# Two weight splits at each layer norm boundary move from GpSimd to VectorE

## The chip, the cores and the metric

One core of one Trainium2 chip runs the whole kernel. The time is the device time of one execution in microseconds, as the median of several runs; smaller is better. TensorE does the matmuls and transposes, VectorE, ScalarE and GpSimd the elementwise work, SyncE issues the transfers.

## The reference

Four layers on 256 tokens of width 1024, all in float32. Each layer is a half-step SwiGLU feed-forward (width 2816), a token mixer (stick-breaking attention, sliding window attention, dilated attention, and stick-breaking again), a second feed-forward, and a gated per-layer input embedding (PLE). The first three end with a layer norm:

```python
for i in range(DEPTH):                       # DEPTH = 4
    x = _layernorm(a * x + 0.5 * _swiglu(x, ffn1_w_in[i], ffn1_w_out[i]), ln_g[i, 0], ln_b[i, 0])
    mix = ...                                # mixer number i % 3
    x = _layernorm(a * x + mix, ln_g[i, 1], ln_b[i, 1])
    x = _layernorm(a * x + 0.5 * _swiglu(x, ffn2_w_in[i], ffn2_w_out[i]), ln_g[i, 2], ln_b[i, 2])
    x = x + jax.nn.sigmoid(x @ ple_w_gate[i]) * (p[i] @ ple_w_proj[i])
```

with `_layernorm(x) = (x - mean) * rsqrt(var + 1e-5) * g + b` over the 1024 columns.

## The kernel before

**Tiles and units.** The 256 tokens are two tiles of 128 (`t` = 0 and 1). Weights are streamed as 730 units of 128 x 1024 numbers (512 KB each) through rings of six slots. To multiply float32 precisely, each unit is split: ScalarE copies `raw` to `wh` in the shorter type fp32r (L446, counted by `hi_done`), then `wl = raw - wh` is computed (L678 on VectorE, counted by `lo_done`). The activations have the same two parts, `xh` and `xl`. TensorE then does three matmuls for each product, wh*xh, wl*xh and wh*xl (L935 to L937). A unit is six matmuls of 512 columns for each tile in most places.

**Stages.** `stages` lists 16 stages in order: ffn1, mixer, ffn2 and PLE for each layer. Each engine runs its own program over them; the order of the work on each is written out by hand, and semaphores tie them. ScalarE splits up to four units (`LEAD`) ahead of the stage that TensorE is in. SyncE loads unit u when `lo_done` says that the slot of unit u - 6 has been split; the loads of the norm's g and b (`norm_load`) stand in the same queue, and wait until the last x of the norm before has been written.

**A boundary.** Behind 12 of the 16 stages (all but PLE) stands a layer norm. On VectorE it is the function `boundary`. For each tile: `residual` (L730) adds the stage's result in two halves of 512 columns, `center` computes the mean (L736) and subtracts it (L741), and `scale` (L750) multiplies by rstd and adds b, one instruction for each half. Between them ScalarE squares and sums (L495), and GpSimd raises to the power -0.5 (L414, L416). `stream_t` makes the next stage's operand: TensorE transposes the half (L978, four transposes), ScalarE copies it to `xh` (L452) and VectorE subtracts to `xl` (L685).

**TensorE at the boundary.** A stage's last four units and the next stage's first four are run by tile. The transposes of tile 0's new x stand before the very last unit of the old stage (tile 1, unit 4 of 4). Behind it come units 0, 1 and 2 of the new stage for tile 0, then the transposes of tile 1's new x, then unit 3 for tile 0, then the four units for tile 1. VectorE's `residual` for tile 1's second half needs that very last unit.

**Who splits here.** Of the four units ahead, `split(2)` in front of `boundary` does units 0 and 1 of the next stage. Units 2 and 3 are split by GpSimd: behind tile 0's rstd its program subtracts `wh` from `raw` for both (L421), once ScalarE has copied them (`split(2)` behind the square of tile 0) and the units before are counted. VectorE skips their numbers (`st["u"] += 2`), and the first split that it does afterwards waits until GpSimd's are counted (`after_pool`). At a PLE stage VectorE does all of them.

Of the kernel before, what the change touches and what calls it, by code (L numbers as in the profile page):

```python
# [20 lines left out]
F32 = mybir.dt.float32  # L21
F32R = mybir.dt.float32r
I32 = mybir.dt.int32
ALU = mybir.AluOpType
# [15 lines left out]
RING = 6  # L40
LEAD = 4
# [34 lines left out]
def steps_of(l):  # L76

    kind = mixer_of(l)
    if kind == "swa":
        return [("q", 0, 0), ("kv", 0, 0), ("q", 1, 0), ("attn", 0, 0), ("attn", 1, 0)]  # L80
    steps = []
    for hh in range(2):
        for g in range(NG if kind == "dil" else 1):
            steps += [("q", hh, g), ("k", hh, g), ("v", hh, g)]
        steps.append(("attn", hh, 0))
    return steps
# [9 lines left out]
def units_of(step):  # L96
    return 2 if step == "kv" else 4


def build_program(nc, A, out):  # L100
    ctx = ExitStack()
    with ctx:
        def sb(name, shape, dt=F32):
            return ctx.enter_context(nc.sbuf_tensor(name, shape, dt))


        raw = sb("raw", [P, RING, UW])
        wh = sb("wh", [P, RING, UW], F32R)
        wl = sb("wl", [P, RING, UW], F32R)
# [78 lines left out]
        def semaphore(name):  # L188
            return ctx.enter_context(nc.semaphore(name))

        landed = [semaphore(f"landed{s}") for s in range(RING)]
        hi_done = semaphore("hi_done")
        lo_done = semaphore("lo_done")
# [37 lines left out]
        stages = []  # L231
        u = 0
        for l in range(DEPTH):
            for kind in ("ffn1", "mix", "ffn2", "ple"):
                n = {"ffn1": 66, "ffn2": 66, "ple": 10, "mix": 8 + sum(units_of(s[0]) for s in steps_of(l) if s[0] != "attn")}[kind]
# [12 lines left out]
        for kind, l, i, u0, n in stages:  # L248
# [49 lines left out]
            if i + 1 < NST:  # L298
                note_stream("x", i + 1)

        norm_index = {i: 3 * l + ("ffn1", "mix", "ffn2").index(kind) for kind, l, i, _, _ in stages if kind != "ple"}

        def wait(eng, sig, *key):
            eng.wait_ge(sig.sem, sig.at(*key))
# [101 lines left out]
        @block.gpsimd  # L406
        def _(pool):
            pool.memset(mhalf[:], -0.5).then_inc(mh_done, 1)
            pool.wait_ge(mh_done, 1)
            for kind, l, i, u0, n in stages:  # L410
                if kind != "ple":
                    for t in range(NT):
                        wait(pool, ssq_done, i, t)
                        pool.tensor_scalar(veps[:, t, :], ssq[:, t, :], 1.0 / D, EPS, ALU.mult, ALU.add).then_inc(mh_done, 1)  # L414
                        pool.wait_ge(mh_done, 2 + 2 * norm_index[i] + t)
                        pool.tensor_tensor(rstd[:, t, :], veps[:, t, :], mhalf[:], ALU.pow).then_inc(rstd_done.sem, 1)  # L416
                        if t == 0:
                            for u in (u0 + n + LEAD - 2, u0 + n + LEAD - 1):
                                pool.wait_ge(hi_done, u + 1)
                                pool.wait_ge(lo_done, u)  # L420
                                pool.tensor_tensor(wl[:, u % RING, :], raw[:, u % RING, :], wh[:, u % RING, :].bitcast(F32),  # L421
                                                   ALU.subtract).then_inc(lo_done, 1)


        @block.scalar
# [231 lines left out]
        def _(dve):  # L657
            st = {"u": 0, "own": 0}

            def own(ins):  # L660

                st["own"] += 1
                ins.then_inc(own_dve, 1)
                dve.wait_ge(own_dve, st["own"])

            after_pool = {u0 + n + LEAD for kind, l, i, u0, n in stages if kind != "ple"}

            def split(n=1, du=0):

                for _ in range(n):  # L670
                    u = st["u"]
                    if u >= UNITS:
                        return
                    st["u"] += 1
                    dve.wait_ge(hi_done, u + 1 + du)
                    if u in after_pool:
                        dve.wait_ge(lo_done, u)
                    dve.tensor_tensor(wl[:, u % RING, :], raw[:, u % RING, :], wh[:, u % RING, :].bitcast(F32),  # L678
                                      ALU.subtract).then_inc(lo_done, 1)

            def stream_t(key, i, t):

                for c in range(2):
                    wait(dve, th_done, key, i, t, c)
                    dve.tensor_tensor(xl[:, 4 * c:4 * c + 4, t, :], ps[:, 2 * t + c, :].rearrange("p (k m) -> p k m", m=P),  # L685
                                      xh[:, 4 * c:4 * c + 4, t, :].bitcast(F32), ALU.subtract).then_inc(tl_done.sem, 1)
# [16 lines left out]
            def ffn(i):  # L703
                split(8)
                hidden(i, 0, BLK)
                with dve.Fori(0, NJ - 1) as r:
                    split(3, r * 12)
                    hidden_t(i, 0, 4, 0, r)
                    split(9, r * 12)
                    hidden(i, 1, BLK, r)  # L710
                st["u"] += 12 * (NJ - 2)
                split(2)
                hidden_t(i, NJ - 1, 4, 0)
                split(2)
                hidden(i, NJ, 256)
                split(2)
                hidden_t(i, NJ, 2, 4)

            def y_wait(kind, i, t, c):

                if t == 0:
                    wait(dve, acc_ready, "y", i, c)
                else:
                    dve.wait_ge(w_used, ends["y", i] - (0 if c else 1 if kind == "ple" else 2))

            def residual(kind, i, t, c):

                y_wait(kind, i, t, c)
                h = slice(c * BLK, (c + 1) * BLK)
                return dve.scalar_tensor_tensor(x[:, t, h], x[:, t, h], ALPHA, ps[:, 4 + 2 * t + c, :], ALU.mult, ALU.add,  # L730
                                                accum_out=rsum[:, t, c:c + 1])

            def center(i, t, ins):

                own(ins)
                dve.tensor_scalar(nmean[:, t, :], rsum[:, t, 0:1], rsum[:, t, 1:2], -1.0 / D, ALU.add, ALU.mult).then_inc(mean_done.sem, 1)  # L736
                wait(dve, mean_done, i, t)
                if t == 0:
                    dve.wait_ge(g_landed, 16 * (norm_index[i] + 1))
                    dve.wait_ge(b_landed, 16 * (norm_index[i] + 1))  # L740
                dve.scalar_tensor_tensor(xn[:, t, :], x[:, t, :], nmean[:, t, :], gb[:, 0, :], ALU.add,  # L741
                                         ALU.mult).then_inc(xn_done.sem, 1)

            def scale(i, t):

                wait(dve, xn_done, i, t)
                wait(dve, rstd_done, i, t)
                for c in range(2):
                    h = slice(c * BLK, (c + 1) * BLK)
                    dve.scalar_tensor_tensor(x[:, t, h], xn[:, t, h], rstd[:, t, :], gb[:, 1, h], ALU.mult,  # L750
                                             ALU.add).then_inc(x_new.sem, 1)

            def embed(i, t):
                for c in range(2):
                    if c == 0:
                        wait(dve, sig_done, i, t)
                    y_wait("ple", i, t, c)
                    h = slice(c * BLK, (c + 1) * BLK)
                    own(dve.tensor_tensor(eg[:, t, h], eg[:, t, h], ps[:, 2 * t + c, :], ALU.mult))
                    dve.tensor_tensor(x[:, t, h], x[:, t, h], eg[:, t, h], ALU.add).then_inc(x_new.sem, 1)  # L760

            def boundary(kind, i):
                more = i + 1 < NST
                if kind == "ple":
                    for t in range(NT):
                        embed(i, t)
                        if t == 0:
                            split(2)
                        if more:
                            stream_t("x", i + 1, t)  # L770
                    return
                residual(kind, i, 0, 0)
                center(i, 0, residual(kind, i, 0, 1))
                scale(i, 0)
                residual(kind, i, 1, 0)
                stream_t("x", i + 1, 0)
                center(i, 1, residual(kind, i, 1, 1))
                st["u"] += 2
                scale(i, 1)
                stream_t("x", i + 1, 1)  # L780

# [577 lines left out]
```

## Time and profile before

| what | value |
|---|---|
| median of 3 runs | 2451.0 us (2448.92 to 2451.81) |
| the profiled execution, first to last instruction | 2447.3 us |
| what lies around that span, against the median | 3.7 us |
| TensorE busy in the span | 2363.5 us, 97% |
| VectorE, ScalarE, GpSimd busy | 1344.2, 1104.6 and 77.8 us |
| mean granted clock of TensorE | 0.967 of full speed |

The profile gives times in us from the start of the span. For the profiled execution only its span is recorded; the three runs are timed as a whole. Busy time of TensorE counts matmuls in flight, also at a lower clock.

### The profile page before, as it was taken

What the parts mean: (1) busy time and instruction counts of PE and PEld (TensorE: products, weight loads), DVE (VectorE), ACT (ScalarE), POOL (GpSimd) and SP (SyncE); (2) the same over time, 40 slices, a digit from 0 to 9 for tenths busy, and PEclk for the clock granted to TensorE, in tenths of its full rate; (3) what the DMA queues carried; (4) which work ended last, traced back from release to release, by engine and by line L of the source; (5) the groups of instructions that cost most, each with busy time, mean ns of one, the idle gap of its engine ahead of it and who ended that gap; (6) DMA issues with size and microseconds to landing.
All of it is one profiled execution on the core that took longest, in us unless ns stands there. A gap on an engine that the chain in (4) does not pass through costs nothing.

```text
span 2447.3 us, 29751 instructions
## 1 busy us (share of the span) xinstructions
PE 2363.5 (97%) x11220; PEld 1943.7 (79%) x11220; DVE 1344.2 (55%) x1634; ACT 1104.6 (45%) x1411; POOL 77.8 (3%) x77
## 2 busy tenths in 40 slices
PE   8999999999999899999999999999999999999998
PEld 7887778878888578878887888787887887777887
DVE  5556355556456465556456655645556546446545
ACT  5444554435344544445344344444444444554443
POOL 0001010010001010010001000000001000001001
PEclk9999999999999589999999999999999999999999
DMA  8555336546654136546655515415554654435562
GB/s 288 187 182 171 97 129 204 179 153 203 201 180 155 35 130 197 180 150 208 196 181 171 180 62 162 148 52 197 186 187 147 207 188 146 164 112 181 174 200 86
DMA packets 212917, 401.21 MB, mean 164 GB/s; under 512 B 12369, under 2 KB 30929, under 8 KB 212689
## 3 DMA queue, kind: packets, MB, share of 16 engines
q1 hardware_dynamic: 212816, 399.83, 50.5%
q8 instruction: 69, 1.13, 0.2%
q14 instruction: 32, 0.25, 0.0%
HBM read 398.73 MB, written 1.05 MB: 163 GB/s over the span
## 4 chain that ended last, share of the span: by engine, by line
PE 92%; DVE 5%; ACT 1%; issue 1%; POOL 0%; DMA 0%; SPq 0%; DVEq 0%; POOLq 0%; ACTq 0%
PE ps L935 27%; PE ps L936 26%; PE ps L937 26%; PE ps L978 5%; DVE x L750 3%; PE ps L1071 2%; PE ps L1101 2%; PE ps L1125 1%; PE ps L1136 1%; DVE wl L678 1%; PE ps L1128 0%; DVE x L730 0%; PE ps L1147 0%; PE ps L1126 0%; ACT arena L495 0%
## 5 line engine op out<-in xcount | busy, mean ns | idle before, releaser
L678 DVE TENSOR_TENSOR wl<-raw,wh 128x1024 fp32r<-128x1024 f32 x706 | 845.3, 1222 | 482.0 <-ACT wh L446 477.4
L446 ACT ACTIVATE wh<-raw 128x1024 fp32r<-128x1024 f32 x730 | 758.0, 1060 | 613.1 <-PE ps L937 595.9
L935 PE MATMUL ps<-wh,xh 128*128 128x512 f32 (+1 forms) x2320 | 890.5, 384 | 5.2 <-DVE xl L685 5.0
L936 PE MATMUL ps<-wl,xh 128*128 128x512 f32 (+1 forms) x2320 | 880.1, 379 | 0.0
L937 PE MATMUL ps<-wh,xl 128*128 128x512 f32 (+1 forms) x2320 | 879.6, 379 | 0.0
L935 PEld LDWEIGHTS ps<-wh,xh 128*128 128x128 f32 x2320 | 441.6, 190 | 87.2 <-DVE xl L685 6.7
L937 PEld LDWEIGHTS ps<-wh,xl 128*128 128x128 f32 x2320 | 440.2, 190 | 82.5
L936 PEld LDWEIGHTS ps<-wl,xh 128*128 128x128 f32 x2320 | 441.2, 190 | 78.8
L935 PE MATMUL ps<-wh,hth 128*128 128x512 f32 x704 | 282.2, 401 | 0.0
L937 PE MATMUL ps<-wh,htl 128*128 128x512 f32 x704 | 278.0, 395 | 0.0
L936 PE MATMUL ps<-wl,hth 128*128 128x512 f32 x704 | 277.9, 395 | 0.0
L935 PEld LDWEIGHTS ps<-wh,hth 128*128 128x128 f32 x704 | 134.4, 191 | 33.2 <-issue 5.8
L937 PEld LDWEIGHTS ps<-wh,htl 128*128 128x128 f32 x704 | 134.4, 191 | 28.7
L691 DVE TENSOR_TENSOR htl<-ps,hth 128x512 fp32r<-128x512 f32 (+1 forms) x96 | 57.6, 642 | 179.6 <-ACT hth L459 179.6
L936 PEld LDWEIGHTS ps<-wl,hth 128*128 128x128 f32 x704 | 134.6, 191 | 25.9
L459 ACT ACTIVATE hth<-ps 128x512 fp32r<-128x512 f32 (+1 forms) x96 | 48.7, 561 | 205.5 <-PE ps L978 205.5
L700 DVE SCALAR_TENSOR_TENSOR arena<-arena,ps 128x512 f32<-128x512 f32 (+1 forms) x96 | 57.5, 640 | 141.0 <-PE ps L937 141.0
L978 PE MATMUL ps<-consts,arena 128*128 128x128 f32 x724 | 105.6, 289 | 5.9 <-DVE arena L849 5.9
L978 PEld LDWEIGHTS ps<-consts,arena 128*128 128x128 f32 x724 | 87.9, 149 | 23.6 <-issue 11.9
L750 DVE SCALAR_TENSOR_TENSOR x<-arena,rstd,gb 128x512 f32<-128x512 f32 x48 | 84.9, 1808 | 23.7 <-POOL rstd L416 23.7
L978 PE MATMUL ps<-consts,x 128*128 128x128 f32 x256 | 43.9, 311 | 55.4 <-DVE x L750 50.6
L452 ACT ACTIVATE xh<-ps 128x512 fp32r<-128x512 f32 x64 | 36.5, 596 | 120.1 <-PE ps L978 119.9
(85 smaller groups left out, 1179.2 us busy)
## 6 DMA issues: line engine op xcount, KB each, us to landing
raw<-in_ffn_w_in SPq DMA_DIRECT2D x352, 512.0 KB, 4.6
raw<-in_ffn_w_out SPq DMA_DIRECT2D x176, 512.0 KB, 4.6
raw<-in_dil_w_in SPq DMA_DIRECT2D x72, 512.0 KB, 4.6
raw<-in_sb_w_in SPq DMA_DIRECT2D x48, 512.0 KB, 4.6
raw<-in_ple_w_gate SPq DMA_DIRECT2D x32, 512.0 KB, 4.3
raw<-in_sb_w_out SPq DMA_DIRECT2D x16, 512.0 KB, 3.8
gb<-in_ln_g SPq DMA_DIRECT2D x12, 512.0 KB, 4.3
gb<-in_ln_b SPq DMA_DIRECT2D x12, 512.0 KB, 5.7
```

The source lines that it names most:

```text
L446: act.activation(wh[:, u % RING, :], raw[:, u % RING, :], ACT.Copy).then_inc(hi_done, 1)
L459: ins = act.activation(hth[:, at:at + n, t, :], ps[:, 2 + t, 0:n * P].rearrange("p (c m) -> p c m", m=P), ACT.Copy)
L678: dve.tensor_tensor(wl[:, u % RING, :], raw[:, u % RING, :], wh[:, u % RING, :].bitcast(F32), ALU.subtract).then_inc(lo_done, 1)
L691: ins = dve.tensor_tensor(htl[:, at:at + n, t, :], ps[:, 2 + t, 0:n * P].rearrange("p (c m) -> p c m", m=P), hth[:, at:at + n, t, :].bitca ...
L700: ins = dve.scalar_tensor_tensor(hb[:, t, 0:n], sg[:, t, 0:n], 0.5, ps[:, 2 + t, 0:n], ALU.mult, ALU.mult)
L750: dve.scalar_tensor_tensor(x[:, t, h], xn[:, t, h], rstd[:, t, :], gb[:, 1, h], ALU.mult, ALU.add).then_inc(x_new.sem, 1)
L935: pe.matmul(out_, a_h, b_h, start=start, stop=False)
L936: pe.matmul(out_, a_h, b_l, start=False, stop=False)
L937: return pe.matmul(out_, a_l, b_h, start=False, stop=stop)
L978: ins = pe.transpose(ps[:, bank + c // 4, (c % 4) * P:(c % 4 + 1) * P], src[:, at + c * P:at + (c + 1) * P], ident)
L1071: ins = pe.matmul(ps[:, bank, at:at + (t + 1) * P], qT[pb:pb + HD, g if kc is None else hh, h // 2, t * P:(t + 1) * P], kT[pb:pb + HD, g, ...
L1101: ins = pe.matmul(opair(h)[pb:pb + HD, t * P:(t + 1) * P], v, eT[:, t * ng + m, :], start=m == 0, stop=m == n - 1)
```

## The change

GpSimd keeps its two small operations for each tile, and no longer splits. VectorE takes both splits itself with the usual `split(2)`, placed behind tile 0's `stream_t` and in front of the `residual` for tile 1's second half. The wait of VectorE for GpSimd's count and the set `after_pool` go. Rings, loads, loops and the other three engines' programs stay.

```diff
@@ gpsimd
                         pool.tensor_tensor(rstd[:, t, :], veps[:, t, :], mhalf[:], ALU.pow).then_inc(rstd_done.sem, 1)
-                        if t == 0:
-                            for u in (u0 + n + LEAD - 2, u0 + n + LEAD - 1):
-                                pool.wait_ge(hi_done, u + 1)
-                                pool.wait_ge(lo_done, u)
-                                pool.tensor_tensor(wl[:, u % RING, :], raw[:, u % RING, :], wh[:, u % RING, :].bitcast(F32),
-                                                   ALU.subtract).then_inc(lo_done, 1)
@@ vector
-            after_pool = {u0 + n + LEAD for kind, l, i, u0, n in stages if kind != "ple"}
-
             def split(n=1, du=0):
...
                     dve.wait_ge(hi_done, u + 1 + du)
-                    if u in after_pool:
-                        dve.wait_ge(lo_done, u)
                     dve.tensor_tensor(wl[:, u % RING, :], raw[:, u % RING, :], wh[:, u % RING, :].bitcast(F32),
                                       ALU.subtract).then_inc(lo_done, 1)
@@ vector, boundary
                 scale(i, 0)
                 residual(kind, i, 1, 0)
                 stream_t("x", i + 1, 0)
+                split(2)
                 center(i, 1, residual(kind, i, 1, 1))
-                st["u"] += 2
                 scale(i, 1)
                 stream_t("x", i + 1, 1)
```

## Rows read from the trace of the kernel before

**Rows 1.** Page, chain that ended last, share of the span by line.
```profile
PE ps L935 27%; PE ps L936 26%; PE ps L937 26%; PE ps L978 5%; DVE x L750 3%; PE ps L1071 2%; PE ps L1101 2%; PE ps L1125 1%; PE ps L1136 1%; DVE wl L678 1%; PE ps L1128 0%; DVE x L730 0%; PE ps L1147 0%; PE ps L1126 0%; ACT arena L495 0%
```

**Rows 2.** Waits: who waited for whom, us in total, times, longest.
```profile
PE ps L978 <- DVE x L750: 50.6, 24, 2.2
```

**Rows 3.** Groups by line, GpSimd: busy us, mean ns.
```profile
L421 POOL TENSOR_TENSOR wl<-raw,wh 128x1024 fp32r<-128x1024 f32 x24 | 59.7, 2486 | 3.0
```

**Rows 4.** Timeline of VectorE, boundary at 758: start us, us.
```profile
758.24 5.67 DVE L750 SCALAR_TENSOR_TENSOR x<-arena,rstd,gb 128x512 f32<-128x512 f32 x2 [0.98 <-POOL rstd L416]
763.83 0.67 DVE L730 SCALAR_TENSOR_TENSOR x<-x,ps 128x512 f32<-128x512 f32 x1
...
764.43 0.68 DVE L685 TENSOR_TENSOR xl<-ps,xh 128x512 fp32r<-128x512 f32 x1
765.74 0.69 DVE L685 TENSOR_TENSOR xl<-ps,xh 128x512 fp32r<-128x512 f32 x1 [0.63 <-ACT xh L452]
767.68 0.69 DVE L730 SCALAR_TENSOR_TENSOR x<-x,ps 128x512 f32<-128x512 f32 x1 [1.24 <-PE ps L937]
...
770.93 1.41 DVE L750 SCALAR_TENSOR_TENSOR x<-arena,rstd,gb 128x512 f32<-128x512 f32 x2 [0.98 <-POOL rstd L416]
...
776.37 2.36 DVE L678 TENSOR_TENSOR wl<-raw,wh 128x1024 fp32r<-128x1024 f32 x2 [1.57 <-ACT wh L446]
```

**Rows 5.** Timeline of ScalarE, same boundary.
```profile
757.12 1.99 ACT L446 ACTIVATE wh<-raw 128x1024 fp32r<-128x1024 f32 x2
761.90 0.60 ACT L452 ACTIVATE xh<-ps 128x512 fp32r<-128x512 f32 x1 [2.79 <-PE ps L978]
```

**Rows 6.** Timeline of TensorE, same boundary.
```profile
758.41 0.39 PE L936 MATMUL ps<-wl,hth 128*128 128x512 f32 x1
758.64 0.39 PE L937 MATMUL ps<-wh,htl 128*128 128x512 f32 x1
761.21 0.66 PE L978 MATMUL ps<-consts,x 128*128 128x128 f32 x4 [2.18 <-DVE x L750]
763.96 1.12 PE L978 MATMUL ps<-consts,x 128*128 128x128 f32 x4 [2.10 <-DVE x L750]
764.73 0.78 PE L935 MATMUL ps<-wh,hth 128*128 128x512 f32 x1
...
767.01 0.63 PE L937 MATMUL ps<-wh,htl 128*128 128x512 f32 x1
767.44 0.63 PE L935 MATMUL ps<-wh,xh 128*128 128x512 f32 x1
...
772.24 1.04 PE L978 MATMUL ps<-consts,x 128*128 128x128 f32 x8
773.03 0.47 PE L935 MATMUL ps<-wh,xh 128*128 128x512 f32 x1
```

**Rows 7.** Timeline of GpSimd, same boundary.
```profile
758.24 5.11 POOL L421 TENSOR_TENSOR wl<-raw,wh 128x1024 fp32r<-128x1024 f32 x2
```

**Rows 8.** Stretches: length, busy by engine, TensorE's granted clock, DMA.
```profile
763.96:768.90 4.94, 4.94 (x14) 4.08 (x15) 3.00 (x8) 0.84 (x2) 0.00 (x0) 0.50 0.00 0
...
2410.72:2414.00 3.28, 3.28 (x11) 2.63 (x9) 1.76 (x5) 0.60 (x1) 0.00 (x0) 0.50 0.52 165
```

**Rows 9.** Timeline of VectorE, two other boundaries.
```profile
1843.24 5.67 DVE L750 SCALAR_TENSOR_TENSOR x<-arena,rstd,gb 128x512 f32<-128x512 f32 x2 [0.98 <-POOL rstd L416]
...
2404.57 5.67 DVE L750 SCALAR_TENSOR_TENSOR x<-arena,rstd,gb 128x512 f32<-128x512 f32 x2 [0.98 <-POOL rstd L416]
```

**Rows 10.** Timeline of TensorE, the same two boundaries, start of unit 3.
```profile
1858.26 0.47 PE L935 MATMUL ps<-wh,xh 128*128 128x512 f32 x1
...
2418.79 0.48 PE L935 MATMUL ps<-wh,xh 128*128 128x512 f32 x1
```

**Rows 11.** Timeline of TensorE, first transposes at two boundaries.
```profile
342.19 1.11 PE L978 MATMUL ps<-consts,x 128*128 128x128 f32 x4 [2.18 <-DVE x L750]
...
1086.01 0.84 PE L978 MATMUL ps<-consts,x 128*128 128x128 f32 x4 [2.18 <-DVE x L750]
```

## The prediction

> **What bounds the kernel now.** I read the chain that ended last first. It lies almost wholly on TensorE, but one VectorE line stands out in it: L750, the scaling that ends a layer norm, has 3% of the span, some 73 us, on the path [rows 1]. The waits say the same from TensorE's side: the longest thing it waits for is that line, 50.6 us in 24 waits of its transposes [rows 2]. The 24 are two at each of the 12 layer norm boundaries. No row of the waits has TensorE waiting for a split, on VectorE or GpSimd, so weights are in time everywhere. The kernel is thus TensorE plus 12 holes, and the change works exactly in these holes. GpSimd's two splits per boundary, 2.49 us each [rows 3], begin in the same instant as L750 does [rows 4, 7].
>
> **One boundary, clocked from L750.** I call 758.24 time 0 and take the boundary there for all, since the twelve look alike. VectorE's L750 is two instructions for tile 0 and takes 5.67 us for them; for tile 1, same shapes and same operation, it takes 1.41 [rows 4]. The only work present at the first and absent at the second is GpSimd's pair, 5.11 us from time 0 [rows 7]; ScalarE converts in the first case too, but only until 0.87 [rows 5]. So the two engines hinder each other by about 5.67 - 1.41 = 4.26 us.
> TensorE's last ordinary matmul starts at 0.40, and the pitch is 0.23 [rows 6]; from 0.63 it has nothing. It transposes x's first half at 2.97, the second at 5.72, runs the closing stage's last unit from 6.49, the next stage's unit 0 from 9.20, units 1 and 2 after it, tile 1's eight transposes at 14.00, and unit 3 from 14.79 [rows 6]. I use the start of unit 3 as the end of the boundary: behind it both traces hold the same work. The boundary where it came earliest has it at 2418.79 - 2404.57 = 14.22, the one where it came latest at 1858.26 - 1843.24 = 15.02 [rows 9, 10]; the mean of the twelve is 14.63.
>
> **The change part by part.**
> *GpSimd's splits go.* L750 for tile 0 then takes what tile 1's takes. Its first half is written at 0.74, the second at 1.41. From one half's end to the transposes TensorE needs 0.13 (the first half of the slow pair ends at 5.67 / 2 = 2.84; transposes at 2.97). So transposes start at 0.87 and 1.54. Four cost 0.40, half of the 0.79 that eight took [rows 6]. The closing unit starts at 1.54 + 0.40 = 1.94 instead of 6.49 and its six matmuls end at 1.94 + 6 x 0.23 = 3.32.
> The Trainium skill, SBUF — State Buffer, section "SBUF: two separate sides", says that VectorE and GpSimd share a port pair which one instruction holds to its end, and that a VectorE operation with two SBUF inputs asks for it against a GpSimd operation that reads SBUF. L750 has two such inputs, and so have the moved splits. By that rule they too would be slow beside GpSimd; by the trace GpSimd has nothing left to do from time 0 until tile 1's rstd, so neither view charges them.
> *VectorE up to the new splits.* The residual of tile 1's first half follows at 1.33 (issue is 0.08 before the pair's end) and takes 0.60 to the next issue [rows 4]. ScalarE is free at 0.87 and copies a half in 0.60, some 0.69 after its transposes begin [rows 5, 6]: 1.56 to 2.16, and, behind the second transposes, 2.23 to 2.83. VectorE's subtractions of xl (0.68 each) run at 2.18 and 2.85, and it is free at 3.46.
> *The two moved splits.* Two splits took 2.36 [rows 4], pitch 1.18. The inputs are there (ScalarE ended them at 0.87). So they run from 3.46 to 5.82. GpSimd had them done at 2.5 and 5.1; unit 2 needs the first at 3.32 + 2 x 1.38 = 6.08, where it is now done at 4.66, and unit 3 needs the second much later. Nothing waits for them on TensorE. SyncE's loads of units 8 and 9 wait for the same count, which comes up to 2.2 us later; before the stages with a norm they stand behind norm_load, which waits for tile 1's x, later still, and a PLE stage has TensorE six units away from them.
> *What stands behind them on VectorE.* This is the price. The residual of tile 1's second half could have run at about 3.4, when the closing unit ends; it now runs at 5.80. From that residual to tile 1's scale it is 3.25 (767.68 to 770.93, with ScalarE's square and GpSimd's power inside [rows 4]), so L750 starts at 9.05 and writes at 9.79 and 10.46. TensorE transposes at 9.92 and 10.59 and starts unit 3 at 10.99. It had finished unit 2 at 3.32 + 3 x 1.38 = 7.46: a new hole of about 2.4 us, owed to the splits. Without them in the way the hole would be nearly gone.
> *Removed waits.* VectorE's and GpSimd's waits for each other's split count cost nothing that a row shows; I take 0. Their upper bound is the time to release an engine, 0.13 a boundary, 1.6 in all.
> *Sum at full clock.* 14.63 - 10.99 = 3.64 a boundary, times 12 = 43.7 us.
>
> **The clock.** The boundary of before held TensorE at half of its 2.4 GHz: granted 0.50 from 763.96 to 768.90, and matmuls at a pitch of 0.43 [rows 6, 8]. That loss is inside the 14.63. After the change the first hole is gone, but the new one of 2.4 is as wide as one of the old ones (2.18). Whether one such hole alone lets the clock fall can be read where the first transposes already ran slow: 1.11 at 342.19 and 0.84 at 1086.01, against 0.66 [rows 6, 11]; that is the case at 3 boundaries (these two are the first and the last), at 9 the clock fell after the second hole. At least a quarter, then, and with a slightly wider hole more; between 0 and 12 I take 6. The price: the shortest low stretch had 3.28 us of busy TensorE at 0.50 in the row shown [rows 8], so half of it, 1.64, rounded up to 1.7 for its edges, is lost; the long one costs 4.94 / 2 = 2.5. Six falls at 1.7 are 10.2 us.
> The Trainium skill, TensorE: Matmul & The Clock Gate, Part 1, says that the gate's schedule runs free of the kernel, so that the same hole may or may not let the clock fall. The trace agrees with its 3 and 9 of 12; it is why I spread over all counts.
>
> **Result.** 43.7 - 10.2 = 33.5 us. The profiled execution spans 2447.3 us; the median of the runs is 2451.0, the 3.7 between is what lies around the span, and I leave it. 2447.3 - 33.5 = 2413.8 of span, 2417.5 us of time.
>
> **The rivals.**
> *No hole lets the clock fall.* The new hole stands alone, where the old ones came in pairs, and 9 of 12 boundaries stood the first. Then 2451.0 - 43.7 = 2407.3.
> *Every hole does.* 12 x 1.7 = 20.4 come back: 2451.0 - 43.7 + 20.4 = 2427.7; with the long fall, 12 x 2.5, 2437.3. Against it: 9 of 12.
> *The weights become the wait.* All of a stage's first loads and splits must come 3.6 us earlier beside unchanged DMA. But the loads behind norm_load hang on tile 1's x and move with it, and the first split behind the boundary ends at 19.3 (776.37 + 1.18 [rows 4]) where unit 4 is wanted at 14.79 + 5 x 1.38 = 21.7. With that slack of 2.4 used up and 1 us lost at each boundary: 2417.5 + 12 = 2429.5.
> *L750 stays slow: the slower case.* If the 5.67 came from something else than GpSimd (ScalarE's work, a bank), the splits would only be a burden. VectorE would be free at 8.11, split until 10.45, run the residual there instead of at 9.44, and all behind it would be 1.01 later: 12 x 1.01 = 12.1 slower, 2463.1. It decides once L750's pair for tile 0 stays above 1.41 + 3.64 = 5.05 us. Against it: GpSimd's 5.11 and the clean 1.41, twelve times over.
> *Nothing changes.* It needs the pair near 5.05 by chance, or a gain that TensorE gives back wholly in the stages; it is busy there without holes.
>
> **How the numbers follow.** Forecast with some falls 0.64; no fall 0.12; falls everywhere 0.12; weights 0.06; slower 0.03; nothing 0.03. The bound between a change and none is 0.2% or 4.9 us, about what this kernel's runs can tell. Faster is 0.94. The range goes from just under the rival without falls, 2405, to just over the weights' rival, 2431; it leaves out the long falls, the slower case and no change.
>
> **What would show it.** L750: 48 instructions at about 0.71 instead of 1.81, and no row of L421; L678 has 24 more, at 1.22. TensorE's transposes at the first tile wait 0.2 to 0.3 instead of 2.18 and 2.10, and at tile 1 for about 2.3, from L750. Unit 3 starts 11.0 after L750's first start. Low clock appears behind tile 1's transposes, at some boundaries. I am wrong if L750's pair for tile 0 is longer than 2, if VectorE's splits are slower than 1.2, if unit 2 waits for L678, or if holes open later in the stages.

## The result, and the profile after

| | before | changed |
|---|---|---|
| median of 4 runs, us | 2449.96 | 2412.03 |
| span of the profiled execution, us | 2447.3 | 2409.6 |
| mean granted clock of TensorE | 0.967 | 0.978 |
| mean of the 12 boundaries, L750's (now L740's) first start to unit 3, us | 14.63 | 11.01 |

The ratio is 0.9846, 95% interval 0.9832 to 0.9860: 37.9 us faster. The forecast was 2417.5 us, with a range of 2405 to 2431. Of the runs below, one of the four executions of "splits only counted" took 3325.0 us at a granted clock of 0.649, and its ratio is worked out without it.

Lines have moved: L740 is `scale` (L750 before), L668 the split (L678), L720 the residual, L731 the centering, L675 the subtraction to xl, L968 the transposes, L925 a first matmul.

The groups by line (busy us, mean ns of one; then idle before them and its releaser), the scaling before and then two lines of the changed kernel:

```profile
L750 DVE SCALAR_TENSOR_TENSOR x<-arena,rstd,gb 128x512 f32<-128x512 f32 x48 | 84.9, 1808 | 23.7 <-POOL rstd L416 23.7
```

```profile
L668 DVE TENSOR_TENSOR wl<-raw,wh 128x1024 fp32r<-128x1024 f32 x730 | 873.9, 1222 | 486.7 <-ACT wh L440 484.0 <-DVE arena L783 0.5
...
L740 DVE SCALAR_TENSOR_TENSOR x<-arena,rstd,gb 128x512 f32<-128x512 f32 x48 | 34.0, 749 | 24.0 <-POOL rstd L416 24.0
```

The mean over the 48 cases of L740 is 749 ns, where it was 1808, and the split costs the same 1222 ns with 24 more of them (706 before). No GpSimd row of the splits (L421 before) is left.

The timeline of VectorE at the same boundary as in [rows 4]; L740 now starts at 748.52:

```profile
748.52 1.42 DVE L740 SCALAR_TENSOR_TENSOR x<-arena,rstd,gb 128x512 f32<-128x512 f32 x2 [0.98 <-POOL rstd L416]
749.86 0.68 DVE L720 SCALAR_TENSOR_TENSOR x<-x,ps 128x512 f32<-128x512 f32 x1
...
750.65 1.36 DVE L675 TENSOR_TENSOR xl<-ps,xh 128x512 fp32r<-128x512 f32 x2
751.93 2.35 DVE L668 TENSOR_TENSOR wl<-raw,wh 128x1024 fp32r<-128x1024 f32 x2
754.20 0.68 DVE L720 SCALAR_TENSOR_TENSOR x<-x,ps 128x512 f32<-128x512 f32 x1
...
757.44 1.41 DVE L740 SCALAR_TENSOR_TENSOR x<-arena,rstd,gb 128x512 f32<-128x512 f32 x2 [0.98 <-POOL rstd L416]
```

Read the last three rows as one sentence: the splits run without a pause from 3.41 to 5.76 after L740's start, the residual starts at 5.68 as they end, and tile 1's L740 follows 3.24 behind the residual. Up to the residual nothing waits for anything but VectorE itself; the 3.24 hold the centering, ScalarE's square and GpSimd's power, for which VectorE waits 0.98.

TensorE at the same boundary, against [rows 6]:

```profile
749.33 1.32 PE L968 MATMUL ps<-consts,x 128*128 128x128 f32 x8
750.41 0.47 PE L925 MATMUL ps<-wh,hth 128*128 128x512 f32 x1
...
758.24 1.97 PE L968 MATMUL ps<-consts,x 128*128 128x128 f32 x8 [2.11 <-DVE x L740]
759.86 0.78 PE L925 MATMUL ps<-wh,xh 128*128 128x512 f32 x1
```

The two old holes are gone: all eight transposes of tile 0 run in one piece at 0.81, and the closing unit starts at 1.89. The new hole has 2.11 us, in front of tile 1's transposes. Here they take 1.97 us and the next matmul 0.78, as in a stretch at half clock; at another boundary, in the same view, they take 1.32 and 0.48:

```profile
2380.04 1.32 PE L968 MATMUL ps<-consts,x 128*128 128x128 f32 x8 [2.11 <-DVE x L740]
2381.12 0.48 PE L925 MATMUL ps<-wh,xh 128*128 128x512 f32 x1
```

The stretches (length, busy time by engine, granted clock, DMA) show it as a number, first behind the boundary at 1624, where the clock fell only after unit 3 had begun, then behind the one shown:

```profile
1636.00:1639.00 3.00, 3.00 (x9) 2.40 (x8) 1.32 (x2) 2.99 (x3) 0.00 (x0) 0.54 1.03 289
759.00:761.50 2.50, 2.50 (x10) 2.21 (x9) 1.31 (x2) 1.83 (x3) 0.00 (x0) 0.50 0.63 197
```

The clock fell at 6 of the 12 boundaries. Unit 3 starts at 10.79 or 10.80 where the clock stayed up (at one of them L740 itself came 0.35 late, and unit 3 at 11.15 by the count of the table), at 10.80 where it fell after unit 3, and at 11.15 to 11.34 at the other five.

### The profile page after: what moved, and what is told of

It reads as the page before. It is cut to its first block, busy times and chain, and to the rows that moved or that the text cites. A ratio compares the mean times of both kernels' runs of the same rounds, so it can differ in the third digit from the quotient of the medians.

```text
span 2409.6 us, 29716 instructions
## 1 busy us (share of the span) xinstructions
PE 2350.5 (98%) x11220; PEld 1929.9 (80%) x11220; DVE 1321.4 (55%) x1658; ACT 1105.4 (46%) x1411; POOL 18.0 (1%) x53
## 3 DMA queue, kind: packets, MB, share of 16 engines
HBM read 398.73 MB, written 1.05 MB: 166 GB/s over the span
## 4 chain that ended last, share of the span: by engine, by line
PE 92%; DVE 5%; ACT 2%; issue 1%; POOL 0%; DMA 0%; SPq 0%; POOLq 0%; DVEq 0%; ACTq 0%
PE ps L925 27%; PE ps L927 26%; PE ps L926 26%; PE ps L968 5%; PE ps L1091 2%; PE ps L1061 2%; DVE wl L668 2%; PE ps L1115 1%; DVE xl L675 1%; PE ps L1126 1%; ACT arena L489 1%; DVE x L740 0%; PE ps L1118 0%; DVE x L720 0%; PE ps L1116 0%
## 5 line engine op out<-in xcount | busy, mean ns | idle before, releaser
L668 DVE TENSOR_TENSOR wl<-raw,wh 128x1024 fp32r<-128x1024 f32 x730 | 873.9, 1222 | 486.7 <-ACT wh L440 484.0
L925 PE MATMUL ps<-wh,xh 128*128 128x512 f32 (+1 forms) x2320 | 888.4, 383 | 5.0 <-DVE xl L675 4.7
L925 PEld LDWEIGHTS ps<-wh,xh 128*128 128x128 f32 x2320 | 440.1, 190 | 85.7 <-DVE xl L675 6.4
L925 PE MATMUL ps<-wh,hth 128*128 128x512 f32 x704 | 278.2, 395 | 0.0
L925 PEld LDWEIGHTS ps<-wh,hth 128*128 128x128 f32 x704 | 132.2, 188 | 32.7 <-issue 5.9
L968 PE MATMUL ps<-consts,arena 128*128 128x128 f32 x724 | 103.9, 286 | 5.9 <-DVE arena L839 5.9
L968 PEld LDWEIGHTS ps<-consts,arena 128*128 128x128 f32 x724 | 86.2, 146 | 23.6 <-issue 11.8
L489 ACT ACTIVATE arena<-x,nmean 128x1024 f32<-128x1024 f32 x24 | 27.7, 1155 | 110.2 <-DVE nmean L726 110.2
L968 PE MATMUL ps<-consts,x 128*128 128x128 f32 x256 | 43.8, 306 | 30.9 <-DVE x L740 25.6
L1061 PE MATMUL ps<-arena 64*128 64x128 f32 (+1 forms) x256 | 64.7, 402 | 8.5 <-DVE nmx L828 8.0
```

The source lines that it names most:

```text
L489: act.activation(sq, x[:, t, :], ACT.Square, bias=nmean[:, t, :], accum_out=ssq[:, t, :]).then_inc(ssq_done.sem, 1)
L925: pe.matmul(out_, a_h, b_h, start=start, stop=False)
L968: ins = pe.transpose(ps[:, bank + c // 4, (c % 4) * P:(c % 4 + 1) * P], src[:, at + c * P:at + (c + 1) * P], ident)
L1061: ins = pe.matmul(ps[:, bank, at:at + (t + 1) * P], qT[pb:pb + HD, g if kc is None else hh, h // 2, t * P:(t + 1) * P], kT[pb:pb + HD, g, ...
```

## The experiments

Each kernel's ratio is to the kernel before, run beside it on the same chip. The changed kernel was timed only in the first set, where the kernel before had 2449.96 us; beside the experiments it had 2448.71, 2448.66 and 2449.61. So a difference of about 1 us from the changed kernel says nothing. "Unit 3" is its mean start over the 12 boundaries, counted from L740's first start (more exactly, from 0.66 after the start of GpSimd's power for tile 0), and "hole" the idle time of TensorE in front of tile 1's transposes, at the boundary that the timelines show (with the needless subtractions, the two in front of tile 0's transposes come first).

| run | us | ratio to before (95%) | unit 3 | hole | falls at the 12 boundaries |
|---|---|---|---|---|---|
| changed kernel | 2412.0 | 0.9846 (0.9832 to 0.9860) | 11.01 | 2.11 | 6 |
| splits only counted | 2382.4 | 0.9724 (0.9706 to 0.9742) | 8.72 | none | 0 |
| needless GpSimd subtractions | 2456.3 | 1.0031 (1.0020 to 1.0042) | 15.25 | 2.03, 2.04 and 0.48 | 12 |
| needless GpSimd memsets | 2413.4 (one run) | | 11.11 | 2.11 | 7 |
| hole filled | 2404.4 | 0.9821 (0.9808 to 0.9834) | 10.83 | filled | 0 |
| GpSimd's splits later | 2397.9 | 0.9789 (0.9774 to 0.9804) | 10.20 | 1.50 | 0 |
| one split moved into the wait | 2413.2 | 0.9856 (0.9841 to 0.9871) | 10.81 | 1.93 | 7 |
| residual first | 2414.1 | 0.9860 (0.9845 to 0.9875) | 11.05 | 2.11 | 6 |
| three moves | 2392.2 | 0.9772 (0.9759 to 0.9785) | 9.80 | 1.03 | 0 |
| VectorE in the wait, one SBUF operand | 2414.5 | 0.9859 (0.9844 to 0.9874) | 11.05 | 2.18 | 7 |
| VectorE in the wait, two SBUF operands | 2427.5 | 0.9917 (0.9902 to 0.9932) | 11.97 | 3.07 | 9 |
| one split on each engine | 2381.2 | 0.9725 (0.9711 to 0.9738) | 8.93 | 0.16 | 0 |

**Splits only counted.** What do the two splits cost where they stand?

```diff
-                split(2)
+                for _ in range(2):
+                    dve.wait_ge(hi_done, st["u"] + 1)
+                    st["u"] += 1
+                    dve.sem_inc(lo_done, 1)
```

> The changed kernel, but VectorE only counts the two moved splits and doesn't compute them, so the low parts of two units per boundary are old data (output not the reference's). Theory: the two splits hold back tile 1's second residual and own the new hole. Residual at 3.4 after L750's first start instead of 5.67, unit 3 at about 8.6 instead of 10.8: 12 x 2.2 = 26 us, and with the hole nearly gone the clock stays up, 10 us more: 2376 us. Rival: something else (TensorE's closing unit, ScalarE, GpSimd's power) sets tile 1's time, the splits are covered: 2412 us, hole still 2.3 us.

Timeline of VectorE, the same boundary (L740 first at 741.31):

```profile
741.31 1.41 DVE L740 SCALAR_TENSOR_TENSOR x<-arena,rstd,gb 128x512 f32<-128x512 f32 x2 [0.99 <-POOL rstd L416]
...
744.85 0.69 DVE L720 SCALAR_TENSOR_TENSOR x<-x,ps 128x512 f32<-128x512 f32 x1
...
748.11 1.41 DVE L740 SCALAR_TENSOR_TENSOR x<-arena,rstd,gb 128x512 f32<-128x512 f32 x2 [0.99 <-POOL rstd L416]
```

The residual comes at 3.54 instead of 5.68, tile 1's L740 at 6.80 instead of 8.92, and unit 3 at 8.72: the new hole belongs to the splits. The time fell by 29.6 us against the changed kernel, where 36 had been expected. The boundaries up to unit 3 gave (11.01 - 8.72) x 12 = 27.5 of it; the 10 that were expected on top for the clock did not arrive as a whole (see "Left open").

**Needless work on GpSimd.** Does GpSimd's reading alone stretch L740?

```diff
+                        if t == 0:
+                            pool.wait_ge(g_landed, 16 * (norm_index[i] + 1))
+                            pool.wait_ge(b_landed, 16 * (norm_index[i] + 1))
+                            for c in range(2):
+                                pool.tensor_tensor(arena[:, 8192 + c * UW:8192 + (c + 1) * UW], gb[:, 0, :], gb[:, 1, :], ALU.subtract)
```

> The changed kernel, with two needless GpSimd subtractions of 128x1024 (gb minus gb, into unused columns of the arena) behind tile 0's rstd; all of the kernel's own work is there. Theory: GpSimd's reading operations alone stretch L750, so tile 0's pair goes from 1.41 back to 5.67 us, and with the splits still on VectorE unit 3 starts near 15.6: 12 x 4.8 = 58 us less the 10 us that clock falls cost already, about 2460 us, slower than the kernel before. Rival: the 5.67 had another source (the rings' slots, the hand-over of counts): the pair stays near 1.4 and the time 2412 us.

Timeline of GpSimd (here the line is L421 again):

```profile
761.88 5.11 POOL L421 TENSOR_TENSOR arena<-gb 128x1024 f32<-128x1024 f32 x2
```

and of VectorE (L745 is `scale` here):

```profile
762.03 5.51 DVE L745 SCALAR_TENSOR_TENSOR x<-arena,rstd,gb 128x512 f32<-128x512 f32 x2 [0.99 <-POOL rstd L416]
...
775.50 1.41 DVE L745 SCALAR_TENSOR_TENSOR x<-arena,rstd,gb 128x512 f32<-128x512 f32 x2 [0.98 <-POOL rstd L416]
```

Two subtractions that touch no ring and raise no count bring the pair back to 5.51, and the kernel is slower than before by 0.2 to 0.4%. In its effect it is the slower rival of the prediction made real. That was priced at 12.1 us above the kernel before; measured are 2456.3 against 2448.7 beside it, 7.6 us.

**Memsets instead.**

```diff
+                        if t == 0:
+                            for c in range(2):
+                                pool.memset(arena[:, 8192 + c * 4 * UW:8192 + (c + 1) * 4 * UW], 0.0)
```

> The changed kernel, with two GpSimd memsets of 128x4096 into unused columns instead of subtractions, several us beside L750. Theory, as the Trainium skill, SBUF - State Buffer, states it for GpSimd operations that read SBUF only: a writing operation doesn't disturb, L750 stays at 1.41 for the pair, 2412 us. Rival: any GpSimd operation of size disturbs, the pair grows by 2 us or more, 2430 us or more.

Timeline of GpSimd, then of VectorE (L743 is `scale` here):

```profile
750.05 7.00 POOL L419 MEMSET arena<- 128x4096 f32 x2
```

```profile
750.21 1.42 DVE L743 SCALAR_TENSOR_TENSOR x<-arena,rstd,gb 128x512 f32<-128x512 f32 x2 [0.98 <-POOL rstd L416]
```

Seven us of writing beside L743, and it takes 1.42. VectorE's two splits, with two SBUF operands as well, start at 753.62 beside the same memsets and take their usual 2.35. GpSimd's being busy does no harm, its subtractions, which read, do. An operation of GpSimd with one operand of this size was not tried. This agrees with the Trainium skill, SBUF — State Buffer, section "SBUF: two separate sides", which limits the conflict of two-input VectorE operations to GpSimd operations that read SBUF.

**Hole filled.** What does the clock cost?

```diff
+            after_norm = {i + 1 for kind, l, i, u0, n in stages if kind != "ple"}
...
                     if (t, n) == (0, 3):
+                        if i in after_norm:
+                            for _ in range(9):
+                                pe.matmul(ps[:, 0 if half1 == 4 else 4, :], xh[:, 0, 0, :], view(wh, (st["u"] - 4) % RING, BLK)[:, 0, :],
+                                          start=True, stop=True)
                         stream_t("x", i, 1)
```

> The changed kernel, with nine needless matmuls of 512 columns (about 2.1 us at full clock) on TensorE in each new hole, into a PSUM bank that nobody reads then; all of the kernel's own work is there. Theory: the hole lets the clock fall at about half of the boundaries at some 1.7 us each, so with the hole filled it stays up: 10 us less, 2402 us, low clock only in the mixers. Rival: the falls cost nothing that counts: 2412 us. If the fill doesn't fit in the hole, a few us more than 2412.

Timeline of TensorE (L1014 is the fill):

```profile
754.70 2.20 PE L1014 MATMUL ps<-wh,xh 128*128 128x512 f32 x9
756.99 1.32 PE L968 MATMUL ps<-consts,x 128*128 128x128 f32 x8
758.07 0.47 PE L925 MATMUL ps<-wh,xh 128*128 128x512 f32 x1
```

Nine needless matmuls at each boundary make the kernel faster by 7.6 us in the medians (7.5 in the profiled spans; 6 by the two ratios, whose intervals just touch). No clock falls at a boundary any more, and the transposes take 1.32 everywhere. The mean clocks fit: time at half clock is 2 x (1 - clock) x span, 106 us in the changed kernel (0.978 of 2409.6) and 91 with the fill (0.981 of 2402.1); half of the 15 us less is 7.5 (the rounding of the clocks leaves some 2 us of doubt in it).

Divided by six falls that would be 1.3 us each, but it is a net number. The price of one fall can be read from boundary to boundary, by VectorE's timeline: a stretch of the changed kernel with a fall at its start, 525.93 to 748.52, then the same stretch with the fill:

```profile
525.93 1.42 DVE L740 SCALAR_TENSOR_TENSOR x<-arena,rstd,gb 128x512 f32<-128x512 f32 x2 [0.98 <-POOL rstd L416]
```

```profile
526.23 1.42 DVE L740 SCALAR_TENSOR_TENSOR x<-arena,rstd,gb 128x512 f32<-128x512 f32 x2 [0.98 <-POOL rstd L416]
...
747.27 1.41 DVE L740 SCALAR_TENSOR_TENSOR x<-arena,rstd,gb 128x512 f32<-128x512 f32 x2 [0.98 <-POOL rstd L416]
```

That is 222.59 against 221.04. The six stretches behind a fall are longer by 1.38 to 1.64 us, 9.0 in all, so a fall costs 1.5; five of the stretches behind no fall agree within 0.06. The third mixer is 1.27 us longer with the fill (337.20 against 335.93, at a granted clock of 0.96 against 0.97) and the first boundary comes 0.36 later, which leaves the 7.5.

**GpSimd's splits later.** The kernel before, with one added wait:

```diff
                             for u in (u0 + n + LEAD - 2, u0 + n + LEAD - 1):
+                                wait(pool, x_new, i, 0, 1)
                                 pool.wait_ge(hi_done, u + 1)
```

> The kernel before, with one wait more: GpSimd's two splits start only when tile 0's x has been written (both halves). Theory: the harm is done to operations that read two tensors in SBUF. L750 for tile 0 is then 1.41, L730 and L685 read one operand from PSUM and aren't touched, but L741 of tile 1 meets the second split and loses up to 2 us; unit 3 near 10.1, fewer clock falls: about 2402 us. Rival: every VectorE operation is held up by GpSimd's, also those with a PSUM operand, and the loss only moves by 1.4 us: 2425 us or more.

Timeline of VectorE (L751 `scale`, L731 residual, L686 xl, L742 centering):

```profile
745.16 1.42 DVE L751 SCALAR_TENSOR_TENSOR x<-arena,rstd,gb 128x512 f32<-128x512 f32 x2 [0.98 <-POOL rstd L416]
746.49 0.68 DVE L731 SCALAR_TENSOR_TENSOR x<-x,ps 128x512 f32<-128x512 f32 x1
...
747.29 1.36 DVE L686 TENSOR_TENSOR xl<-ps,xh 128x512 fp32r<-128x512 f32 x2
...
749.69 2.98 DVE L742 SCALAR_TENSOR_TENSOR arena<-x,nmean,gb 128x1024 f32<-128x1024 f32 x1
753.47 1.42 DVE L751 SCALAR_TENSOR_TENSOR x<-arena,rstd,gb 128x512 f32<-128x512 f32 x2 [0.80 <-POOL rstd L416]
```

GpSimd splits from 746.65 to 751.59. Beside that, L731 and L686, which have a PSUM operand, take 0.68 and 1.36 as always; L742, with x and gb both in SBUF, takes 2.98 instead of 1.28. Timeline of GpSimd:

```profile
746.65 4.94 POOL L422 TENSOR_TENSOR wl<-raw,wh 128x1024 fp32r<-128x1024 f32 x2 [1.61 <-DVE x L751]
751.68 1.05 POOL L414 TENSOR_SCALAR veps<-ssq 128x1 f32<-128x1 f32 x1
```

L414, which handles one number per partition, takes 1.05 here and 0.19 elsewhere; the next experiment explains it. One wait added to the old kernel is worth 51 us, more than the change itself.

**Moves within VectorE's order.** First the second split alone into VectorE's wait for rstd:

```diff
-                split(2)
+                split(1)
                 center(i, 1, residual(kind, i, 1, 1))
+                split(1)
                 scale(i, 1)
```

> The changed kernel, with the second of the two splits moved behind the center of tile 1 (L741), where VectorE waits about 1 us for rstd. Theory: tile 1's second residual runs 1.18 us sooner, the split fills the wait and overruns it by 0.2: unit 3 starts 0.95 us sooner, 11 us, and the hole falls to 1.4 us, which hardly lets the clock fall, up to 10 us: 2391 us. Rival: the order of the splits doesn't matter because what follows hangs on GpSimd's power: 2412 us.

It gained nothing that can be measured. Timeline of VectorE, then of GpSimd:

```profile
754.72 1.22 DVE L668 TENSOR_TENSOR wl<-raw,wh 128x1024 fp32r<-128x1024 f32 x1
756.74 1.41 DVE L740 SCALAR_TENSOR_TENSOR x<-arena,rstd,gb 128x512 f32<-128x512 f32 x2 [0.79 <-POOL rstd L416]
```

```profile
754.85 1.14 POOL L414 TENSOR_SCALAR veps<-ssq 128x1 f32<-128x1 f32 x1 [6.95 <-ACT arena L489]
756.08 0.55 POOL L416 TENSOR_TENSOR rstd<-veps,mhalf 128x1 f32<-128x1 f32 x1
```

Here GpSimd's L414 starts 0.13 behind the split and takes 1.14, to 0.05 after its end. My theory had counted VectorE's time and not what VectorE does to GpSimd: 1.15 us were gained in front of the centering, 0.95 lost on rstd.

Second, the residual of tile 1's first half ahead of tile 0's L740 (`residual(kind, i, 1, 0)` and `scale(i, 0)` exchanged):

> The changed kernel, with the residual of tile 1's first half placed ahead of tile 0's L750, where VectorE waits 1 us for rstd. Theory: 0.6 us of work leaves the stretch behind L750, but L750 itself starts 0.1 to 0.2 later; TensorE's closing unit loses that, unit 3 gains 0.4 to 0.5: 5 us, 2407 us. Rival: the residual isn't ready in time (TensorE has to finish three of tile 1's four units first) and L750 is late by as much as is gained: 2412 us.

The rival held: L740 starts 0.08 late, and the stretch behind it is no shorter, since the subtractions to xl wait for ScalarE there anyway (2.21 against 2.13).

Third, both of them, and the first split right behind L740, where now a gap is:

```diff
-                scale(i, 0)
                 residual(kind, i, 1, 0)
+                scale(i, 0)
+                split(1)
                 stream_t("x", i + 1, 0)
-                split(2)
                 center(i, 1, residual(kind, i, 1, 1))
+                split(1)
                 scale(i, 1)
```

> Three moves at once: the residual of tile 1's first half ahead of tile 0's L750, one split right behind L750 (ahead of tile 0's subtractions), the other behind tile 1's L741. Theory: the residual of tile 1's second half runs near 4.0 instead of 5.67, unit 3 near 9.2 instead of 10.8, the hole is under 1 us and the clock stays up: 12 x 1.6 = 19 us and 10 us, 2383 us. Rival: the split ahead of the subtractions makes unit 0 late on TensorE (xl near 3.3, wanted at 3.3) and eats it: 2400 us.

It gave 20 us of the 29 expected: unit 3 at 9.80 instead of 9.2, because L414 takes 1.14 here too. The hole of 1.03 let no clock fall.

**One or two operands in the wait.** The two next runs measure that effect by itself, with one line added to the changed kernel between `center` and `scale` of tile 1; the operand in the middle is `ps[:, 6:8, :]`, flattened, in the first and `gb[:, 1, :]` in the second, which is shown:

```diff
                 center(i, 1, residual(kind, i, 1, 1))
+                dve.tensor_tensor(arena[:, 8192:8192 + UW], gb[:, 1, :], gb[:, 0, :], ALU.subtract)
                 scale(i, 1)
```

> The changed kernel, with one needless VectorE subtraction of 128x1024 (a PSUM operand and gb, into unused columns) between L741 and L750 of tile 1, in the wait for rstd. Theory, from the run with one split each side, where GpSimd's small L414 took 1.14 us instead of 0.19: it was a VectorE operation reading two SBUF tensors that held GpSimd up. This one reads only one there, so L414 stays at 0.19, and L750 starts later only by what the operation outlasts the wait, 0.2 to 0.3 us: 12 x 0.25 = 3 us, 2415 us. Rival: any VectorE operation in that place delays GpSimd, then as the next run.

> The same with both operands in SBUF (gb and gb). Theory: GpSimd's L414 finds the port taken and takes 1.1 us, rstd and with it L750 of tile 1 come 0.9 to 1.0 us later, unit 3 too: 12 x 0.95 = 11 us, 2423 us. Rival (L414's 1.14 was no contention but ScalarE's sum arriving late): no difference from the run before.

Timeline of GpSimd with the PSUM operand, then with both in SBUF:

```profile
757.60 0.19 POOL L414 TENSOR_SCALAR veps<-ssq 128x1 f32<-128x1 f32 x1 [8.08 <-ACT arena L489]
```

```profile
762.22 1.15 POOL L414 TENSOR_SCALAR veps<-ssq 128x1 f32<-128x1 f32 x1 [8.08 <-ACT arena L489]
```

Both added operations take 1.22 us and stand in the same place. The first leaves L414 at 0.19 and costs no measurable time; the second makes it 1.15, moves tile 1's L740 from 8.98 (8.92 in the changed kernel) to 9.86, and costs 13 us against the first, two more clock falls included.

**One split on each engine.** VectorE splits one unit where GpSimd is idle, GpSimd the other where VectorE works out of PSUM. Against the kernel before:

```diff
-                            for u in (u0 + n + LEAD - 2, u0 + n + LEAD - 1):
+                            for u in (u0 + n + LEAD - 1,):
...
-                scale(i, 0)
                 residual(kind, i, 1, 0)
+                scale(i, 0)
+                split(1)
                 stream_t("x", i + 1, 0)
                 center(i, 1, residual(kind, i, 1, 1))
-                st["u"] += 2
+                st["u"] += 1
```

> Both engines, never at the same time as a two-input partner: the residual of tile 1's first half ahead of tile 0's L750, VectorE's one split right behind L750, GpSimd's one split behind that, from 2.6 to 4.7, beside VectorE's subtractions and residual with PSUM operands and just ahead of L741. Theory: the second residual runs at 3.74, L414 is 0.19, tile 1's L750 starts at 7.0, unit 3 at 8.9 and no hole lets the clock fall: the time of the run that leaves the splits out, 2382 us, 10 us under the best version so far. Rival: GpSimd's split still meets L741 or loses to the subtractions, so that L741 takes 2 us or more: 2392 us or more.

Timeline of VectorE, then of GpSimd:

```profile
742.44 1.41 DVE L750 SCALAR_TENSOR_TENSOR x<-arena,rstd,gb 128x512 f32<-128x512 f32 x2
743.76 1.22 DVE L678 TENSOR_TENSOR wl<-raw,wh 128x1024 fp32r<-128x1024 f32 x1
744.90 1.28 DVE L685 TENSOR_TENSOR xl<-ps,xh 128x512 fp32r<-128x512 f32 x2
...
747.07 1.55 DVE L741 SCALAR_TENSOR_TENSOR arena<-x,nmean,gb 128x1024 f32<-128x1024 f32 x1
749.40 1.42 DVE L750 SCALAR_TENSOR_TENSOR x<-arena,rstd,gb 128x512 f32<-128x512 f32 x2 [0.78 <-POOL rstd L416]
```

```profile
745.13 2.41 POOL L421 TENSOR_TENSOR wl<-raw,wh 128x1024 fp32r<-128x1024 f32 x1 [2.89 <-DVE wl L678]
748.40 0.27 POOL L414 TENSOR_SCALAR veps<-ssq 128x1 f32<-128x1 f32 x1 [0.86 <-ACT arena L495]
```

GpSimd's split fits into the gap but for its last 0.47 us, which L741 pays with 0.27. Unit 3 starts at 8.93, and 2381.2 us is, within the noise, what the kernel takes that leaves the two splits out (2382.4). It is the fastest version of the study that does all the work, 31 us under the changed kernel.

## Why the prediction was right

**The bound and the removed conflict.** Right: L750's pair went from 5.67 to 1.42, forecast 1.41. The added subtractions on GpSimd show the cause, the memsets narrow it to operations of GpSimd that read, and the later splits show VectorE operations with a PSUM operand free of it. One sign of being wrong was badly set: "slower than 1.2" for a split, when one took 1.22 before and after.

**The chain behind it.** Each step of the working against the profile, counted from L740's first start: closing unit 1.94 forecast, 1.89 measured; splits 3.46 and 3.41; residual 5.80 and 5.68; tile 1's L740 9.05 and 8.92; unit 3 at full clock 10.99 and 10.79; idle before the transposes about 2.3 and 2.11. Of the residual's 0.12, 0.06 are a slip: VectorE's next operation starts 0.08 before the end of the pair before it, as the prediction says itself, so splits that end at 5.82 give 5.74 and not 5.80. That the moved splits own this hole is shown by the run that only counts them.

**The clock.** Six falls were forecast and six measured; the forecast was the middle of an open range, so the number itself is partly luck. The price was set at 1.7 each; from boundary to boundary, against the filled hole, it is 1.5. The term was sized as if the whole low stretch were matmuls. Part of it is tile 1's transposes, and eight of these lose only 0.54 (next matmul 1.62 behind their start at 758.24, against 1.08 at 2380.04), a third of their time and not half.

**The sum.** At full clock 12 x (14.63 - 10.79) = 46.1 us, forecast 43.7; the span fell by 37.7, so 8.4 came back, forecast 10.2 (six falls at the measured 1.5 make 9.0). The forecast span was 2413.8 and came out 2409.6; 2.4 of these 4.2 are the chain's 0.2 per boundary, 1.8 the clock's term. The other 1.3 of the 5.5 between 2417.5 and 2412.0 lie around the span: I had put 3.7 there, the difference between a median and one execution's span, and it is 2.4 by the same measure in the changed kernel (1.95 for the profiled execution itself, 2411.55 against 2409.6).

**The rivals.** By the time alone, the rival without falls (2407.3) lay nearer to 2412.0 than the forecast did. Its mechanism did not happen, six falls did; the filled hole shows what its time would have been, 2404.4. No wait for weights came up: no row of TensorE's waits names L668. The slower case didn't happen; with GpSimd's reading put back beside L750 it costs 7.6 us against the kernel before, where 12.1 was the price.

**What the prediction didn't see.** It says that the two engines hinder each other, but in all its steps only VectorE pays. GpSimd pays as well, and the place that the change chose for the splits, before the residual and not in the wait for rstd, happens to avoid it. The prediction got its numbers right without knowing that.

Left open: what low clock inside the mixers owes to the boundaries. From the run that only counts the splits 10 us were expected for the clock, and 29.6 - 12 x (10.79 - 8.69) = 4.4 came. From boundary to boundary it reads so: the six falls gave their 9.0 back, and 5.1 were lost again, 1.2, 1.3 and 1.8 in the second, third and fourth mixer and 0.7 ahead of the first boundary. The fourth mixer ran at a mean granted clock of 0.96 there, against 0.99 in the changed kernel. Why the clock falls there in one run and not in the other, I didn't separate.

## What to carry to other kernels

A busy engine off the critical path can cost more than its work is worth when it slows another: compare the duration of one operation at places with and without the neighbour at work. Here a line with 1.41 us at one tile and 5.67 at the other was the clue. Before work is moved into a wait, ask what the engine that is waited for does then. And place the work of the two by their operands: in this kernel, VectorE's operations with two operands in SBUF where GpSimd reads nothing, and GpSimd's subtraction beside VectorE's operations with a PSUM operand. With one split on each engine in these places, and a residual moved ahead, it was 31 us faster than with both on VectorE.

## What the runs showed of the hardware

- GpSimd's reading operations and VectorE's operations with two SBUF operands hold each other up, in both directions: L750's pair 1.41 to 5.67, L741 1.28 to 2.98, GpSimd's one-number L414 0.19 to 1.15. A GpSimd memset of 7.0 us beside L743 changed nothing, and VectorE's operations with a PSUM operand were not slowed (0.68 and 1.36) and did not slow L414 (0.19).
- Needless matmuls in a hole made the kernel faster, 2404.4 against 2412.0 us, with the granted clock at the full level (2.4 GHz) at all 12 boundaries instead of 6. A fall cost 1.38 to 1.64 us.
- Behind holes of 0.16, 1.03 and 1.50 us before tile 1's transposes the clock fell to half at none of the 12 boundaries, behind 1.93 at seven, 2.11 at six or seven (three kernels), 2.18 at seven, 3.07 at nine.
